# A chunked scan: the products of a round grouped by tile shape, and its operands laid out by chunk

## The reference, cut to what matters

```python
def step(s, inp):
    r_t, w_t, k_t, v_t, kk_t, a_t = inp
    sa = jnp.einsum('bhvk,bhk->bhv', s, -kk_t)
    s = (s * w_t[:, :, None, :] + sa[..., None] * (kk_t * a_t)[:, :, None, :]
         + v_t[..., None] * k_t[:, :, None, :])
    return s, jnp.einsum('bhvk,bhk->bhv', s, r_t)
```

## Time and profile before

| | |
|---|---|
| time, median of 3 runs | 4100.36 us (4093.78 to 4100.76) |
| the profiled execution | 4094.72 us, its span 4092.9 us |
| busy: PE, DVE, ACT, POOL | 3684.4 us (90%), 2350.2 (57%), 1910.5 (47%), 1215.6 (30%) |
| mean granted TensorE clock | 0.943 of full speed |
| stage `scan` | from 1121 us to about 2295 us of the span |

### The profile page before, as it was taken

The page is one execution under the profiler, slowest core; times in us unless marked ns, Lnnn a source line. Parts: engine busy times, 40 slices in busy tenths (PEclk is TensorE's granted clock), DMA queues, the critical chain, the costliest instruction groups (busy, mean ns, idle before and its releaser), DMA issues. The chain is left out here.

```text
span 4092.9 us, 93137 instructions
## 1 busy us (share of the span) xinstructions
PE 3684.4 (90%) x39677; PEld 3199.6 (78%) x39677; DVE 2350.2 (57%) x4331; ACT 1910.5 (47%) x2991; POOL 1215.6 (30%) x1222
## 2 busy tenths in 40 slices
PE   5699999999978898988989688897599999999997
PEld 2578888888767777777778588675499999999986
DVE  3236666640046766766667655343666666667676
ACT  3335666641145665665656444232244443444454
POOL 1223333331045555555553255101001010111102
PEclk7799999999989999999999799898699999999999
DMA  5235555542264454444442466343367676666786
GB/s 172 62 120 176 179 180 169 176 148 75 69 127 87 94 107 82 91 106 86 96 85 47 155 217 188 119 145 122 101 203 213 205 212 205 201 216 206 235 278 218
DMA packets 771394, 611.33 MB, mean 149 GB/s; under 512 B 267618, under 2 KB 698532, under 8 KB 769956
## 3 DMA queue, kind: packets, MB, share of 16 engines
q1 hardware_dynamic: 721828, 493.84, 42.2%
q0 software_dynamic: 22688, 80.75, 6.6%
q10 hardware_dynamic: 26464, 30.77, 2.5%
HBM read 443.62 MB, written 161.50 MB: 148 GB/s over the span
## 5 line engine op out<-in xcount | busy, mean ns | idle before, releaser
L579 PE MATMUL moe_h<-moe_xt_hi,moe_w_hi 128*128 128x256 f32 x2048 | 583.2, 285 | 7.9 <-DVE moe_w_lo L431 4.0
L431 DVE TENSOR_TENSOR moe_w_lo<-moe_w_lo_whole,moe_w_hi 128x2048 fp32r<-128x2048 f32 x254 | 446.3, 1757 | 243.4 <-ACT moe_w_hi L647 196.5
L579 PE MATMUL moe_h<-moe_xt_hi,moe_w_lo 128*128 128x256 f32 x2048 | 580.9, 284 | 0.0
L579 PE MATMUL moe_h<-moe_xt_lo,moe_w_hi 128*128 128x256 f32 x2048 | 580.9, 284 | 0.0
L1963 PE MATMUL inward_pp<-u_u_hi,inward_w_hi 128*128 128x512 f32 (+1 forms) x1360 | 527.9, 388 | 20.4 <-POOL inward_w_lo L2123 20.4
L1963 PE MATMUL inward_pp<-u_u_lo,inward_w_hi 128*128 128x512 f32 (+1 forms) x1360 | 516.3, 380 | 0.0
L1963 PE MATMUL inward_pp<-u_u_hi,inward_w_lo 128*128 128x512 f32 (+1 forms) x1360 | 516.0, 379 | 0.0
L579 PEld LDWEIGHTS moe_h<-moe_xt_hi,moe_w_hi 128*128 128x128 f32 x2048 | 394.1, 192 | 19.0 <-issue 5.9
L579 PEld LDWEIGHTS moe_h<-moe_xt_lo,moe_w_hi 128*128 128x128 f32 x2048 | 394.2, 192 | 3.6
L579 PEld LDWEIGHTS moe_h<-moe_xt_hi,moe_w_lo 128*128 128x128 f32 x2048 | 394.1, 192 | 0.0
L487 POOL DMA_INDIRECT scratch_x<-moe_ys,moe_who x30 | 86.1, 2870 | 867.0 <-DVE moe_ys L753 748.5
(11 more groups left out here) (386 smaller groups left out, 8929.7 us busy)
## 6 DMA issues: line engine op xcount, KB each, us to landing
moe_w_lo_whole<-in_moe_w SPq DMA_DIRECT2D x384, 512.0 KB, 5.1
scratch_ops<-inward_ops SPq DMA_DIRECT2D x72, 512.0 KB, 3.8
scan_by_parity<-scratch_ops SPq DMA_DIRECT2D x144, 192.0 KB, 6.4
inward_w_lo_whole<-in_w_in SPq DMA_DIRECT2D x38, 512.0 KB, 4.5
scan_aq<-scratch_ops SPq DMA_DIRECT2D x72, 256.0 KB, 4.9
scan_kb<-scratch_ops SPq DMA_DIRECT2D x36, 512.0 KB, 5.7
scratch_gates<-inward_out SPq DMA_DIRECT2D x64, 256.0 KB, 2.1
all_late<-in_w_mod POOLq DMA_DIRECT2D x32, 512.0 KB, 5.2
```

The costliest lines, as they stand in the source:

```text
L431: return nc.vector.tensor_tensor(x_lo, x, x_hi.bitcast(F32), ALU.subtract)
L579: mm = nc.tensor.matmul(hb[ft % 2][m][:, 0:CAP], w_, x_, start=(k == 0 and part == 0), stop=(k == KD - 1 and part == 2))
```

## The change

In `inward` the buffer `o` becomes three: B and K; A and Q with the chunks side by side (64 numbers of A, 64 of Q, and so on); the decays. In DRAM A and Q of a chunk are neighbours and the decays follow them, so that `aq` with the decays is one DMA of 4128 bytes a partition. `store_ops` issues three DMAs for a direction where it issued two.

In `scan` `kb` goes; `ob` (B, 256 KB) and `over` (K, A and Q with the two heads of a pair on exchanged partitions, 768 KB in two DMAs) take its place. `joint` replaces `side_by_side`: in `begin(1)` B of pair 0 runs on its two quarters while K of pair 1, read from `over`, runs on the other two, whose outputs land on the right partitions; in `begin(2)` K of pair 0 and B of pair 1. Both wait for both pairs. Step S runs its parts K, Q and S for both pairs each, so all 64x128 products with K, then all 64x64 ones, then all 64x128 ones with Z; one start flag per bank. The state update is two VectorE instructions with a scalar from `aq` in place of one with a broadcast operand. H has two buffers in place of three. `undecayed` and `large` take over memory of constants no longer used.

```diff
@@ inward
-                    sp.dma_start(slots, o[:, d, 0:O_PEND].rearrange("p (x t) -> p x t", t=G)).then_inc(s_o, 16)
-                    sp.dma_start(place(i, d)[:, 10 * G + 4 * d:10 * G + 4 * d + 4], o[:, d, O_PEND:]).then_inc(s_o, 16)
+                    sp.dma_start(to[:, AT_B:AT_AQ].rearrange("p (x d t) -> p x d t", d=2, t=G)[:, :, d, :], o_bk[:, :, d, :]).then_inc(s_o, 16)
+                    sp.dma_start(to[:, AT_AQ + 2 * G * d:AT_AQ + 2 * G * (d + 1)], o_aq[:, d].rearrange("p c x t -> p (c x t)")).then_inc(s_o, 16)
+                    sp.dma_start(to[:, AT_END + 4 * d:AT_END + 4 * d + 4], o_end[:, d, :]).then_inc(s_o, 16)
@@ scan, SP
-                        for x in range(2):
-                            sp.dma_start(aq[u][:, it % 2, :, x, :], by_chunk(src[:, (6 + 2 * x) * G:(8 + 2 * x) * G])).then_inc(s_aq[u][it % 2], 16)
-                        sp.dma_start(till_end[u][:, it % 2, :], src[:, 10 * G:OPS]).then_inc(s_aq[u][it % 2], 16)
+                        sp.dma_start(aq[u][:, it % 2, :], src[:, AT_AQ:OPS]).then_inc(s_aq[u][it % 2], 16)
                     if rest:
-                        sp.dma_start(kb[u][:, :, :].rearrange("p x t -> p (x t)"), src[:, 2 * G:6 * G]).then_inc(s_kb[u], 16)
+                        sp.dma_start(ob[u][:, :], src[:, AT_B:AT_K]).then_inc(s_ob[u], 16)
...
+                        for part, head in zip(HALVES, HALVES[::-1]):
+                            sp.dma_start(over[u][part, :], src[head, AT_K:AT_END]).then_inc(s_over[u], 16)
@@ scan, TensorE
+            def beside(u, k, lhs, rhs, across):
+                for h, other in zip(HALVES, HALVES[::-1]):
+                    to = bank[u][2 + k // 4][other if across else h, k % 4 * P:(k % 4 + 1) * P]
+                    mm = nc.tensor.matmul(to, lhs[h, k * HD:(k + 1) * HD], rhs[h, k * P:(k + 1) * P], start=True, stop=True)
+                return mm
+
+            def joint(r, a):
+                it, b, half = a
+                uB, uK = (0, 1) if r == 1 else (1, 0)
+                for u in U:
+                    if r == 1:
+                        AC[u].wait(pe, "V", it)
+                    else:
+                        DV[u].wait(pe, EVICTED[FIRST_OF[u][0]][1] + "1", it)
+                pe.wait_ge(s_over[uK], 32 * it + 32)
                 for k in range(8):
...
+                    mmB = beside(uB, k, ob[uB], aq[uB][:, b, :], False)
+                    mmK = beside(uK, k, over[uK], over[uK][:, 2 * G:], True)
+                PE[uB].did("B", mmB)
+                PE[uK].did("K", mmK)
...
-                        DV[u].wait(pe, "Lk1", it)
+                        DV[u].wait(pe, second_done[u], it)
...
+                elif step == "K":
+                    ACg.wait(pe, "ri"[u], 4 * it + c)
+                    DVc[u].wait(pe, f"Z{c}", it)
+                    for d, x in every:
+                        mm = nc.tensor.matmul(sum_of(d, x, WHOLE), both(byK, d, x), blk(V, d, x), start=(d == 0), stop=False)
+                elif step == "Q":
+                    for d, x in every:
+                        h = HALVES[x]
+                        mm = nc.tensor.matmul(sum_of(d, x, HALVES[1]), own_of(u, h, b, 4 * d + at[d], 1), S[u][h, c % 2, d, :], start=False, stop=False)
                 else:
...
+                    for d, x in every:
+                        mm = nc.tensor.matmul(sum_of(d, x, WHOLE), both(byB, d, x), Z[u][HALVES[x], d, :], start=False, stop=(d == 1))
...
-                    for part in step:
+                    for part in ("KQS" if step == "S" else step):
                         for u in U:
                             state(u, chunk, part, c)
@@ scan, VectorE
+                    product = FIRST_OF[u][r - 1]
+                    PE[u].wait(dve, product, it)
...
-                    gain = till_end[u][:, b, c:8 - c:7 - 2 * c].unsqueeze(2).broadcast_to([P, 2, HD])
-                    D.did(f"S{c}", dve.tensor_tensor(S[u][:, (c + 1) % 2, :, :], undecayed[u][:, :, :], gain, ALU.mult))
+                    for d, at in ((0, c), (1, 3 - c)):
+                        gain = aq[u][:, b, 4 * G + 4 * d + at:4 * G + 4 * d + at + 1]
+                        D.did(f"S{'ab'[d]}{c}", dve.tensor_scalar(S[u][:, (c + 1) % 2, d, :], undecayed[u][:, d, :], gain, None, ALU.mult))
@@ scan, GpSimd
-                    elif m > 3:
-                        PE[u].wait(pool, f"F{m - 3}", it)
-                    PO[u].did(f"H{m}", pool.tensor_tensor(four(H[u][(m - 1) % 3][:, :, :]), four(L[u][:, :, :]), masked(f"lev{m}t"), ALU.mult))
+                    elif m == 2:
+                        if it:
+                            PE[u].wait(pool, "F4", it - 1)
+                    else:
+                        PE[u].wait(pool, f"F{m - 2}", it)
+                    PO[u].did(f"H{m}", pool.tensor_tensor(four(H[u][(m - 1) % 2][:, :, :]), four(L[u][:, :, :]), masked(f"lev{m}t"), ALU.mult))
```

More of the change, by code:

```diff
@@ L1803, in inward @@
         kka = n.sb("kka", [P, 2, G])
-        o = n.sb("ops", [P, 2, 4 * G + 4])
+        o_bk = n.sb("ops_bk", [P, 2, 2, G])
+        o_aq = n.sb("ops_aq", [P, 2, NJ, 2, HD])
+        o_end = n.sb("ops_end", [P, 2, NJ])
+        o_b, o_k = (o_bk[:, x, :, :] for x in range(2))
+        o_a, o_q = (o_aq[:, :, :, x, :] for x in range(2))
         half = n.sb("half", [P, 6 * NJ])
@@ L2298, in scan @@
         V, La, byK = twice("V"), twice("La"), twice_beside("tK_Lk")
-        kb = each("kb", [P, 4, G])
+        over = each("over", [P, 6 * G])
+        ob = each("ob", [P, 2 * G])
         xp = each("by_parity", [P, 12, 2, HD])
@@ L2343, in scan @@
         ACc = steps("act_state", chunks(["X", "Y"]))
-        DVc = steps("dve_state", chunks(["Z", "Ua", "Ub", "S"]))
+        DVc = steps("dve_state", chunks(["Z", "Ua", "Ub", "Sa", "Sb"]))
         s_aq = [[n.sem(f"aq{u}{b}") for b in range(2)] for u in U]
-        s_kb, s_xp = ([n.sem(f"{x}{u}") for u in U] for x in ("kb", "by_parity"))
+        s_ob, s_over, s_xp = ([n.sem(f"{x}{u}") for u in U] for x in ("b", "over", "by_parity"))
         lru = lambda name, names: Steps(n.sem(f"lru_{name}"), names)
@@ L2459, in decayed @@
                     for h in HALVES:
-                        mm = nc.tensor.matmul(bank[u][2][h, k * HD:(k + 1) * HD], aq[u][h, b, k, 0, :],
-                                              kb[u][h, 2 + k // 4, k % 4 * HD:(k % 4 + 1) * HD], start=True, stop=True)
+                        mm = nc.tensor.matmul(bank[u][2][h, k * HD:(k + 1) * HD], own_of(u, h, b, k, 0), ob[u][h, k * HD:(k + 1) * HD], start=True, stop=True)
                 PE[u].did("L", mm)
@@ L2507, in forward @@
                     AC[u].wait(pe, "tK", it)
-                held, old = of(H[u][(m - 1) % 3]), of(W[u])
+                held, old = of(H[u][(m - 1) % 2]), of(W[u])
                 for pos in range(4):
```

122 lines of the change are left out of this document (51 added, 71 removed).

## The result

The changed kernel takes 4156.98 us, median of 4 runs (4148.39 to 4163.44), beside 4100.56 us of the kernel before, measured with it: ratio 1.0135, 95% interval 1.0108 to 1.0162. It is slower by 56 us; the forecast was 3966 us, in a range of 3910 to 4045. The profiled execution took 4148.39 us, its span 4146.4 us at a granted clock of 0.925.

The account below looks back on a forecast made before the run. TensorE was taken to set the pace in projection and scan. 26 + 31 + 4 + 48 + 20 + 2 = 131 us off the profiled 4094.7 gave 3964; half the 5.6 us to the median added: 3966 us, range 3910 to 4045.

Parts of the forecast that it names:

- The loads of `over`: Scan: 0.5 MB more per pair and round, two DMAs issued mid-round some 35 us ahead of use; no cost counted.
- The joint products: Products B and K on four quarters: 1.9 us a pass, 2.3 us standstill before the second; 26 us gain (0 to 43).
- the second rival: Joint passes no faster, since two heads writing one bank take turns: 30 us less gain, 3996 us; chance 0.09.
- the first rival: Standstill before the second joint pass lowers the clock, the joint takes 2.5 us: 80 us off, about 4018; chance 0.12.
- GpSimd: Later W of pair 1 shifts the H run to 12 to 17 us; first H at 13.3, before 14.1.
- Two H buffers: H4 waits for the second forward pass, H5 for the third, each over 10 us ahead of use: no cost.
- The split update: VectorE's state update as two instructions for one, 0.1 to 0.3 us each without waiting, counted as the one.
- The fourth rival: Each half of the split state update may wait for a GpSimd instruction: 3 us a round slower, 4150; chance 0.06.
- Step S: Scan, grouping by shape: 2.65 us a step for 3.56; 31 us gain (22 to 37), 4 us more in the tail.
- The load wait: TensorE's wait for operands opening a round: of 58.8 us about 10 stay; 48 us gain (30 to 58).
- The start of the stage and the stores: With `over`, +2 us (-3 to 5) gain; 72 more stores in the projection stage covered by TensorE there.
- The clock: Scan's granted clock rises above 0.93 as the opening wait goes: 20 us gain (-15 to 45); below 0.90 means wrong.

Follow-up runs that it names:

- e19: e14 without joint products and without the loads of `over`: 4052.46 us.
- e22: e14 with exactly its loads, `over` included, but each product by itself, K read out of `over`: 4107.22 us.
- e14: Changed kernel with the addition to W of pair 1 behind H1 and H2 on GpSimd and the state's decay on ScalarE: 4113.61 us.
- e23: e14 with the loads of `over` issued after the third forward pass: 4088.02 us.
- e4: Changed kernel without joint products and `over`, B then K for both pairs from one load: 4090.64 us.
- e18: e4 with GpSimd's addition to W of pair 1 waiting for the masks of that pair's second product: 4132.83 us.
- e11: e16 with the grouped step S added (three H buffers, one instruction for the decay): 4051.82 us.
- e10: e11 with two H buffers in place of three: 4077.41 us.
- e5: e4 with three H buffers in place of two, split state update kept: 4109.77 us.
- e16: Kernel before with only the operands laid out by chunk in DRAM, a pair's decays and queries in one load: 4061.53 us.
- e1: Changed kernel with the addition to W of pair 1 moved behind H1 and H2 on GpSimd: 4143.24 us.
- e12: Changed kernel with GpSimd's mask products H left out but for one column each, output not the reference's: 4090.03 us.

## Why the prediction was wrong, step by step

**The loads of `over` (two DMAs more, "in the middle of a round, some 35 us ahead of their use").** Of the steps that could be measured alone this one has the largest error. It was priced at nothing, by the mean DMA share of 0.45 and by how far ahead the loads are issued. Both hold: after the first round no pass waits for `over`, and the mean share is 0.47. But the loads come right behind those by parity, and the engines are full for some 15 us (share 1.11 from 1668.5 to 1683.5), while TensorE's instructions come the same way. Price where it could be measured alone: 55 us (e19 to e22); in the kernel with joint products 26 come back by moving the loads (e14 to e23). The prediction had read a mean where the DMA's share in that stretch was wanted.

**The joint products.** 1.9 us were forecast for a pass; the first takes 2.1 and the second, at full clock, 1.9: right, and the second rival (banks, taking turns) is out. The standstill of 2.3 us: right, 2.42 in each round. What was missed is the clock behind it. Second pass and step S were to take 4.5 us together; they do in eight of the 17 rounds (4.6 to 5.0), and take 6.1 to 7.6 in the nine in which the clock falls, 5.7 on the mean. From B to the turning the forecast had 1.7 us less; on the mean it was 11.2 before and 11.0 after, 9.8 to 10.2 in the eight good rounds. That is the first rival's mechanism, in half of the rounds. In the mended frame the joint order by itself costs 6 us (4107.2 to 4113.6; the intervals overlap) where 26 were forecast as a gain.

**GpSimd ("it fits by 0.8 us").** It was asked whether H would be ready for the forward pass; it was. What was not asked is what VectorE does from 12 to 17 us: the recurrences, slower beside it (mean of the scan instruction 774 ns before, 1210 after, 745 without H). A late W alone costs 42 us in e4 (e18). The sentence that VectorE is busy without a gap and gains little named the right place and had the wrong sign.

**Two H buffers ("nothing").** 26 us (e11 to e10), but -19 beside the split update (e5 to e4). The split update, counted as the old one: 13 us with two H buffers, 58 with three, 2 in the changed kernel. The fourth rival came nearest to the time, 4150, but by another cause.

**Step S.** 2.65 us forecast, 2.69 measured. Worth 41 us in the changed kernel (31 and 4 forecast), but 10 where the layout alone had been changed. The Trainium skill, TensorEngine Tiling (Array Packing), section Tiling Modes, has it that a change of the tiling mode drains the engine; the trace agrees, with a step 0.87 us shorter for two changes of shape inside it in place of eight.

**The load wait.** 58.8 to 7.3 us, so 51 less where 48 were forecast; median landing of the one load 4.8 us. Yet the layout alone brings 37 us, not 48 and 20 for the clock: the other waits, for VectorE and ScalarE, grow from 36 us to 42, and those for nothing shown from 9 to 26 (between 1190 and 2180 us, before and e16).

**The start of the stage and the stores.** The 72 stores cost nothing, as forecast: 850.08 of 857 us. The start was to gain 2 us and lost 7: the first round ends at 1190.7 us where it ended at 1183.4.

**The clock.** Forecast above 0.93 for the stage, measured 0.87, below the 0.90 that the prediction named as a sign of being wrong; a round takes 66.3 us where 54 to 57 were forecast. A standstill isn't always followed by the lower level: the one of 2.42 us before the second pass is in nine rounds of 17. Of the 16 waits of over 1 us for the copy of Z, all but one (2.02 us) are followed by 4.6 us at a mean clock of 0.50 to 0.62. The change put both into nearly every round where it took away one in some rounds.

**The sum.** The prediction had 131 us of gain, and the kernel lost 56. The layout and the grouping gain 47 us together; the three parts with a price of nothing (buffers, split update, loads) and the joint order take 105. How the 66 us of the last step divide between loads, late W and standstill in the changed kernel itself stays open: alone they are worth 55, 42 and some 6 in other frames, so they overlap. It speaks for an overlap that the loads there start at 1668.50 and TensorE stands still from 1673.6 to 1677.0 for the copy of Z anyway, and that its stops for nothing shown doubled when e1 took that wait away; this is argued, not shown. That the loads alone cost the same in the changed kernel's own frame was not run.

## What to carry to other kernels

Price an added load by how full the DMA engines are in the stretch in which it lands, not by the mean: where they were full here, even an engine that needed none of the data stopped, since its instructions came late, and the lower clock behind the stops cost more than the stops (2.3 and 1.3 us a round, e19 to e22). When work is moved on one engine, ask what every other engine does at the new time, not only whether the result is still in time. And a buffer given up for space can have a price: undo it by itself, and beside the other edits, since the price here was 26 us in one frame and -19 in another.

## What the runs showed of the hardware

TensorE's instructions, about 65 bytes each, come through a DMA queue of their own, some 2.6 MB in 990 us, and it stopped for up to 5.0 us (e12, DMA share 1.28 in that stop) where operand loads filled the engines. Of 343 such stops in 20 traces 342 ended 1.2 to 1.9 us after a 16 KB packet of that queue. The same standstill of 2.42 us was followed by full clock in eight rounds and by the lower level in nine. VectorE's update of the state is held up by GpSimd's instructions beside it as long for 64 columns as for 128: 254 ns at the median and 1348 at the most for 64, 644 ns on the mean in e5 and 631 for 128 in e11. The Trainium skill, SBUF — State Buffer, section Who interferes with whom, names the pair of ports that VectorE shares with GpSimd; the trace agrees, with 745 ns for the scan instruction where the H run is gone and 1210 where it lies beside.
